# Convolution and pooling mixer of a two-block transformer kernel: taps accumulated in PSUM, three input groups on four banks, pooled channels first in the output product

## The reference

```python
def conv_pool_mixer(h, w_in, dw_w, dw_b, ln_g, ln_b, pool_w, pool_scale, w_out):
    z = h @ w_in                                   # 1024 -> 3 x 512
    a_val, a_gate, u = z[..., :512], z[..., 512:1024], z[..., 1024:]
    a = a_val * jax.nn.sigmoid(a_gate)
    a = causal_depthwise_conv(a, dw_w, 31 taps) + dw_b
    a = jax.nn.silu(layernorm(a, ln_g, ln_b))
    # u in 4 groups of 128 channels, windows 2, 4, 8, 16
    pooled = windowed_mean(u)                      # sum of the window / count
    p = einsum('btgc,gcd->btgd', pooled - u, pool_w) * pool_scale
    return jnp.concatenate([a, p], axis=-1) @ w_out   # 1024 -> 1024
```

## Time and profile before

| | us |
|---|---|
| median of 3 runs | 1901.66 |
| lowest and highest | 1900.48, 1903.46 |
| profiled execution, its own time | 1900.42 |
| its span in the trace | 1898.6 |
| PE busy | 1816.5 (96%) |
| DVE busy | 868.1 (46%) |
| ACT busy | 616.8 (32%) |
| POOL busy | 728.3 (38%) |

### The profile page before, as it was taken

The page is one execution under the profiler, slowest core; times in us unless marked ns, Lnnn a source line. Parts: engine busy times, 40 slices in busy tenths (PEclk is TensorE's granted clock), DMA queues, the critical chain, the costliest instruction groups (busy, mean ns, idle before and its releaser), DMA issues.

```text
span 1898.6 us, 24087 instructions
## 1 busy us (share of the span) xinstructions
PE 1816.5 (96%) x8442; PEld 1476.1 (78%) x8442; DVE 868.1 (46%) x1392; ACT 616.8 (32%) x814; POOL 728.3 (38%) x315
## 2 busy tenths in 40 slices
PE   8899989999999885999999999999999999999998
PEld 6788777888888773588888888888888788888886
DVE  2544446333333689642323324656657333242325
ACT  5444434222222430443222223434243342222223
POOL 3122224444444447245343544323233245444341
PEclk9899999999999997999999999999999999999999
DMA  9711112233232121033232323212122133323231
GB/s 199 121 56 56 56 56 89 89 99 102 97 99 93 61 74 56 20 103 100 78 110 88 106 93 93 84 46 77 55 66 66 45 111 100 99 88 99 79 109 45
DMA packets 149494, 159.78 MB, mean 84 GB/s; under 512 B 9892, under 2 KB 110872, under 8 KB 149440
## 3 DMA queue, kind: packets, MB, share of 16 engines
q1 hardware_dynamic: 148911, 158.79, 28.1%
q10 hardware_dynamic: 528, 0.26, 0.0%
HBM read 156.40 MB, written 2.62 MB: 84 GB/s over the span
## 4 chain that ended last, share of the span: by engine, by line
PE 49%; issue 29%; POOL 10%; DVE 7%; ACT 3%; DMA 1%; SPq 1%; POOLq 0%; DVEq 0%; ACTq 0%
PE ps L1017 43%; POOL wlo L562 10%; DVE conv L1822 3%; PE ps L1299 2%; PE ps L1166 1%; PE ps L1155 1%; DMA bias_rows<-relrow 1%; DVE ss L1498 1%; DVE acc L1519 0%; PE ps L1130 0%; PE ps L1131 0%; DVE h_lo L1486 0%; POOL wlo L573 0%; DMA raw<-in_w_in 0%; ACT whi L631 0%
## 5 line engine op out<-in xcount | busy, mean ns | idle before, releaser
L562 POOL TENSOR_TENSOR wlo<-raw,whi 128x1024 fp32r<-128x1024 f32 x272 | 657.6, 2431 | 1076.7 <-ACT whi L631 1062.8
L1017 PE MATMUL ps<-h_hi,wlo 128*128 128x512 f32 x1472 | 590.6, 401 | 15.8 <-POOL wlo L573 7.4
L1017 PE MATMUL ps<-h_hi,whi 128*128 128x512 f32 x1472 | 576.8, 392 | 0.0
L1017 PE MATMUL ps<-h_lo,whi 128*128 128x512 f32 x1472 | 575.7, 391 | 0.0
L631 ACT ACTIVATE whi<-raw 128x1024 fp32r<-128x1024 f32 x282 | 292.2, 1054 | 523.3 <-PE ps L1017 504.1
L1017 PEld LDWEIGHTS ps<-h_hi,wlo 128*128 128x128 f32 x1472 | 278.0, 189 | 79.1 <-POOL wlo L573 8.3
L1017 PE MATMUL ps<-m_hi,wlo 128*128 128x512 f32 x800 | 319.9, 400 | 4.2 <-DVE m_lo L1649 1.6
L1017 PEld LDWEIGHTS ps<-h_hi,whi 128*128 128x128 f32 x1472 | 277.3, 188 | 59.5
L1017 PEld LDWEIGHTS ps<-h_lo,whi 128*128 128x128 f32 x1472 | 278.1, 189 | 57.8 <-issue 2.9
L1017 PE MATMUL ps<-m_lo,whi 128*128 128x512 f32 x800 | 317.1, 396 | 0.0
L1017 PE MATMUL ps<-m_hi,whi 128*128 128x512 f32 x800 | 317.0, 396 | 0.0
(11 more groups left out here) (238 smaller groups left out, 1401.0 us busy)
## 6 DMA issues: line engine op xcount, KB each, us to landing
raw<-in_ffn_w SPq DMA_DIRECT2D x264, 256.0 KB, 2.9
raw<-in_w_ff SPq DMA_DIRECT2D x128, 256.0 KB, 2.9
raw<-in_hg_w_in SPq DMA_DIRECT2D x64, 256.0 KB, 3.3
raw<-in_w_in SPq DMA_DIRECT2D x40, 256.0 KB, 5.5
raw<-in_cp_w_in SPq DMA_DIRECT2D x24, 256.0 KB, 3.0
raw<-in_w_out SPq DMA_DIRECT2D x16, 256.0 KB, 2.9
raw<-in_cp_w_out SPq DMA_DIRECT2D x16, 256.0 KB, 2.9
raw<-in_hg_w_out SPq DMA_DIRECT2D x16, 256.0 KB, 2.8
```

The source lines that it names most:

```text
L562: pool.tensor_tensor(wlo[:, u % RING, :, :], raw[:, u % RING, :, :], whi[:, u % RING, :, :].bitcast(F32), ALU.subtract).then_inc(unit_lo, 1)
L1017: mm = pe.matmul(ps[:, b, :], wt[:, s, a, m * P:(m + 1) * P], xt[:, kts[a], :], start=starts and a == 0 and i == 0, stop=last)
```

## The change

In the mixer alone:

1. The taps of tiles 0, 1 and 2 accumulate in PSUM (banks 4, 5 and 6, the odd half sum of tile 2 in bank 4 once tile 0 is done): each step reads `apad` from SBUF and the running sum from PSUM, and writes to PSUM; the last step writes to `conv` in SBUF. As no PE or ACT instruction uses these banks meanwhile, DVE counts them up itself (`release`).
2. For that, the three input groups all use banks 0 to 3, in the order g = 0, 2, 1, and the tap matmuls and the variance use bank 7.
3. DVE takes the pooled input out one bank at a time ahead of steps 10 to 13, and the gates and values of group 1 tile by tile ahead of steps 24 to 29, tile 3 first; PE computes group 1 in the order 3, 1, 2, 0.
4. PE starts the taps of tile 3 when tile 3 alone is gated, does 16 taps, all four pool products, and the other 15; then output unit 0, the mean, output unit 1, the variance, and output units 2 to 7. `CPOUT_ORDER` puts all four units of pooled channels first, for both halves of the outputs, and SP loads in that order.
5. POOL does the low parts of units 8 to 11 before the windows, and of output units 0 to 2 after them. ACT splits one more unit before the first sigmoids, and scales the pool products before the bias of tile 3. The pool products are scaled into `pdiff` in place of the half of `late`, which still holds the tap matrices.

```diff
+CPOUT_ORDER = ((0, 4), (0, 6), (1, 4), (1, 6), (0, 0), (0, 2), (1, 0), (1, 2))
...
-    b.stage("cpin", [(("g", 0, m), m) for m in range(4)] + [(("g", 2, m), 4 + m) for m in range(4)]
-            + [(("g", 1, m), m) for m in range(4)] + [("conv", 4), ("mean", 5)]
-            + [(("pool", j), 6 + j % 2) for j in range(4)] + [("var", 4)])
+    b.stage("cpin", [(("g", g, m), m) for g in (0, 2, 1) for m in range(4)] + [(("pool", j), j) for j in range(4)]
+            + [(("taps", j), 4 + j) for j in range(3)] + [("odd", 4), ("mean", 5), ("conv", 7), ("var", 7)])
...
-            odd = sb("odd", [P, SEQ], scope=s)
...
-        csq, pout = late[:, 0:4, :], late[:, 4:8, :]
+        csq, pout = late[:, 0:4, :], pdiff
...
-            for h in range(2):
-                for j, kts in enumerate(order):
-                    load(U_CPOUT, 4 * h + j, pieces("cp_w_out_2", kts, h * COLS))
+            for j, (h, kt) in enumerate(CPOUT_ORDER):
+                load(U_CPOUT, j, pieces("cp_w_out_2", (kt, kt + 1), h * COLS))
...
-            lo_part(U_CPIN + 8)
-            lo_part(U_CPIN + 9)
+            for j in range(8, 12):
+                lo_part(U_CPIN + j)
...
-                if j < 3:
-                    lo_part(U_CPIN + 10 + j)
-            for j in range(1, 3):
+            for j in range(3):
                 lo_part(U_CPOUT + j)
...
             inv_rms(4)
-            for g in range(2):
-                if g:
-                    for j in range(4, 12):
-                        split(U_CPIN, j)
...
+            split(U_CPIN, 4)
+
+            def sigmoid_of(g, i):
+                b = banks.bank("cpin", ("g", g, 2 + i))
+                act.wait_ge(drained[b], nth("cpin", ("g", g, 2 + i)))
+                act.activation(csig[:, i, :], csig[:, i, :], ACT.Sigmoid).then_inc(csig_ready, 1)
+
+            sigmoid_of(0, 0)
+            sigmoid_of(0, 1)
+            for j in range(5, 12):
+                split(U_CPIN, j)
+            split(U_CPOUT, 0)
+            sigmoid_of(1, 1)
+            sigmoid_of(1, 0)
...
-            act.wait_ge(filled[4], nth("cpin", "conv"))
...
             for j in range(4):
                 pool_out(j)
             act.preload_act_table_set(LOG_TABLES)
+            act.wait_ge(filled[7], nth("cpin", "conv"))
+            c = COL["cp_dw_b_2"] + 3
+            act.activation(conv[:, 3, :], bank("cpin", "conv"), ACT.Identity, bias=vecs[:, c:c + 1])\
+                .then_inc(drained[7], 1)
+            split(U_CPOUT, 1)
...
-            split(U_CPOUT, 1)
-            act.wait_ge(filled[4], nth("cpin", "var"))
+            split(U_CPOUT, 2)
...
-                .then_inc(drained[4], 1)
-            act.wait_ge(drained[4], nth("cpin", "var"))
+                .then_inc(drained[7], 1)
+            act.wait_ge(drained[7], nth("cpin", "var"))
...
-            for j in range(2, 6):
+            for j in range(3, 6):
                 split(U_CPOUT, j)
...
-            gates_first = (2, 3, 0, 1)
-            group(U_CPIN, 0, "cpin", [("g", 0, m) for m in range(4)], order=gates_first, n=2, between=norm_after(4, 3))
+            group(U_CPIN, 0, "cpin", [("g", 0, m) for m in range(4)], order=(2, 3, 0, 1), n=2, between=norm_after(4, 3))
             group(U_CPIN, 4, "cpin", [("g", 2, m) for m in range(4)])
-            group(U_CPIN, 8, "cpin", [("g", 1, m) for m in range(4)], order=gates_first)
+            group(U_CPIN, 8, "cpin", [("g", 1, m) for m in range(4)], order=(3, 1, 2, 0))
...
+            def conv_taps(lo, hi):
+                for i in range(lo, hi):
+                    mm = pe.matmul(bank("cpin", "conv"), tapdiag[:, i, :], apad[:, 3, i:i + SEQ],
+                                   start=i == 0, stop=i == TAPS - 1)
+                    if i == TAPS - 1:
+                        mm.then_inc(filled[7], 1)
+
+            def cpout(j):
+                h, kt = CPOUT_ORDER[j]
...
+                unit(U_CPOUT, j, m_hi, m_lo, (kt, kt + 1), "cpout", [("h", h, m) for m in range(4)], kt == 4, kt == 2,
+                     wait_tile=tile if j in (4, 5) else None, by_tile=kt == 2)
+
+            pe.wait_ge(drained[7], before("cpin", "conv"))
+            pe.wait_ge(tapdiag_ready, 1)
+            pe.wait_ge(apad_ready, 3)
+            conv_taps(0, 16)
             pe.wait_ge(poolw_in, 16)
-            pool_product(0)
-            pool_product(1)
-
-            pe.wait_ge(drained[4], before("cpin", "conv"))
-            pe.wait_ge(tapdiag_ready, 1)
-            pe.wait_ge(apad_ready, 4)
-            for i in range(TAPS):
-                mm = pe.matmul(bank("cpin", "conv"), tapdiag[:, i, :], apad[:, 3, i:i + SEQ],
-                               start=i == 0, stop=i == TAPS - 1)
-            mm.then_inc(filled[4], 1)
+            for j in range(4):
+                pool_product(j)
+            conv_taps(16, TAPS)
+            pe.wait_ge(pout_lo, 2)
+            cpout(0)
             pe.wait_ge(drained[5], before("cpin", "mean"))
             pe.wait_ge(csum_step, 3)
             pe.matmul(bank("cpin", "mean"), ones[:, :], csum[:, :], start=True, stop=True).then_inc(filled[5], 1)
-            pool_product(2)
-            pool_product(3)
-            pe.wait_ge(pout_lo, 2)
-            out_unit(U_CPOUT, "cpout", 0)
-            pe.wait_ge(drained[4], before("cpin", "var"))
+            pe.wait_ge(pout_lo, 4)
+            cpout(1)
+            pe.wait_ge(drained[7], before("cpin", "var"))
             pe.wait_ge(csum_step, 6)
-            pe.matmul(bank("cpin", "var"), ones[:, :], csum[:, :], start=True, stop=True).then_inc(filled[4], 1)
-            pe.wait_ge(pout_lo, 4)
-            out_unit(U_CPOUT, "cpout", 1)
+            pe.matmul(bank("cpin", "var"), ones[:, :], csum[:, :], start=True, stop=True).then_inc(filled[7], 1)
             for j in range(2, 8):
-                if j < 4:
-                    pe.wait_ge(cs_lo, 2 * j - 2)
-                out_unit(U_CPOUT, "cpout", j)
+                cpout(j)
...
-            def gates(g):
...
-            def gated(g):
...
+            def gate_in(g, i):
+
+                b = banks.bank("cpin", ("g", g, 2 + i))
+                dve.wait_ge(filled[b], nth("cpin", ("g", g, 2 + i)))
+                dve.tensor_tensor(csig[:, i, :], ps[:, b, :], rs[:, :], ALU.mult).then_inc(drained[b], 1)
...
+            def value_in(g, i):
+
+                b = banks.bank("cpin", ("g", g, i))
+                dve.wait_ge(filled[b], nth("cpin", ("g", g, i)))
+                dve.tensor_tensor(apad[:, 2 * g + i, PAD:], ps[:, b, :], rs[:, :], ALU.mult).then_inc(drained[b], 1)
...
+            def gated(g, i, count):
+
+                b = banks.bank("cpin", ("g", g, i))
+                dve.wait_ge(drained[b], nth("cpin", ("g", g, i)))
+                dve.wait_ge(csig_ready, count)
+                dve.tensor_tensor(apad[:, 2 * g + i, PAD:], apad[:, 2 * g + i, PAD:], csig[:, i, :], ALU.mult)\
+                    .then_inc(apad_ready, 1)
...
+            def pool_in(m):
+                b = banks.bank("cpin", ("g", 2, m))
+                dve.wait_ge(filled[b], nth("cpin", ("g", 2, m)))
+                dve.tensor_tensor(upad[:, m, POOL_PAD:], ps[:, b, :], rs[:, :], ALU.mult).then_inc(drained[b], 1)
...
+            def release(b):
+
+                dve.sem_inc(filled[b], 1)
+                dve.sem_inc(drained[b], 1)
...
-                a, w_i = apad[:, j, i:i + SEQ], taps[:, i, j:j + 1]
+                a, w_i, b = apad[:, j, i:i + SEQ], taps[:, i, j:j + 1], banks.bank("cpin", ("taps", j))
                 if i == 0:
-                    dve.tensor_scalar(conv[:, j, :], a, w_i, col("cp_dw_b_2", j), ALU.mult, ALU.add)\
+                    dve.wait_ge(drained[b], before("cpin", ("taps", j)))
...
                     dve.wait_ge(tap_done[j], i)
-                    dve.scalar_tensor_tensor(out=conv[:, j, :], in0=a, scalar=w_i, in1=conv[:, j, :], op0=ALU.mult,
-                                             op1=ALU.add).then_inc(tap_done[j], 1)
-
...
+            gate_in(0, 0)
+            gate_in(0, 1)
+            value_in(0, 0)
+            value_in(0, 1)
+            gated(0, 0, 1)
+            gated(0, 1, 2)
...
             for i in range(TAPS):
-                if i == 13:
-
-                    for m in range(4):
-                        b = banks.bank("cpin", ("g", 2, m))
-                        dve.wait_ge(filled[b], nth("cpin", ("g", 2, m)))
-                        dve.tensor_tensor(upad[:, m, POOL_PAD:], ps[:, b, :], rs[:, :], ALU.mult).then_inc(drained[b], 1)
+                if 10 <= i < 14:
+                    pool_in(i - 10)
+                if i == 24:
+                    gate_in(1, 1)
+                if i == 25:
+                    value_in(1, 1)
                 if i == 26:
-                    gates(1)
+                    gate_in(1, 0)
                 if i == 27:
-                    gated(1)
+                    gated(1, 1, 3)
+                    value_in(1, 0)
+                if i == 29:
+                    gated(1, 0, 4)
                 tap(0, i)
```

(74 more changed lines are left out.)

14 lines of the change are left out of this document (5 added, 9 removed).

## The result

| us | before | after |
|---|---|---|
| median of 4 runs | 1902.23 (1900.48 to 1903.46) | **1879.78** (1878.69 to 1880.58) |
| profiled execution, its own time | 1900.42 | 1879.24 |
| its span | 1898.6 | 1877.5 |
| PE busy | 1816.5 | 1815.7 |
| DVE busy | 868.1 | 840.3 |

After takes 0.9882 of the time of before, 95% interval 0.9865 to 0.9899. The forecast was 1878, range 1872 to 1889. PE does the same work as before; it merely stands idle less.

A forecast was written before the change was run, and what follows sets the result against it. PE, busy 96%, was taken to bound the kernel, idling while DVE's taps took turns with POOL. GLU start moves from 831.30 to 807.5, gaining 23.8: 1900.4 becomes 1876.6, plus 1.2 for the median, forecast 1878 us, range 1872 to 1882.

The forecast's parts named there:

- (g): PE's clock falling after two new waits of 2.6 and 3.4 us: charged 1.6 and 1.8 us, end 807.5.
- p: Time between starts of two DVE tap steps in PSUM: taken as 0.66 us, bounds 0.60 and 1.35.
- Rival B: DVE steps slower, as reading and writing one bank might not stream together: p = 1.18, 1911 us; chance 0.06.
- C: DVE steps in between, p of 0.85 to 1.0: 1878 to 1892 us before any clock loss; chance 0.06.
- (a): Four banks for three groups: PE's pooled input waits for bank 0 until 677.3, ends at 699.2, 2.6 us later.
- (b): Pooled input taken out bank by bank: bank 3 free at 701.8, PE idles 2.6 us before group 1.
- (c): Gating tile 3, with 0.8 us for POOL: PE begins its taps at 727.0 instead of 750.35, idle 3.4 us.
- (d): PE's taps and products of tile 3: together 30.1 us, end 757.1; the output unit after them ends at 762.7.
- (e): DVE's work meanwhile: the mean could start at 758.7, before PE is ready; covered up to p = 0.79.
- (f): Mean to GLU: 41.4 us, the norm hidden by two pooled-channel units, without which PE would wait 10; end 804.1.
- Rival A: DVE's turns with POOL stay: mean near 780, gain 9 us less clock, 1893 us; chance 0.08.

The follow-up runs named there:

- after_again: The changed kernel as it is, run once more for comparison: 1879.83 us, ratio 0.988 to before.
- Kernel c: The changed kernel with ACT's split of output unit 4 put behind the inverse root: 1876.73 us, ratio 0.9861 to before.
- a: The changed kernel, taking the pooled input out ahead of and between the taps of two steps instead of four: 1879.09 us, ratio 0.987 to before.

## Why the prediction was right, and where its parts were not

All times from DVE's first take of a gate, as forecast (less 675.42) and as the trace of after has them:

| event | forecast | measured |
|---|---|---|
| first unit of the pooled input | 2.0 | 2.0 |
| group 1 starts | 26.4 | 26.6 |
| PE's taps of tile 3 start (clock charge of g in it) | 53.2 | 52.8 |
| mean | 90.7 | 88.7 |
| GLU starts | 132.1 | 131.5 |

**p, the step in PSUM.** I took 0.66 between 0.60 and 1.35. It is 0.66, and the bounds have their reasons now: 18 steps took 11.94 us in PSUM and 12.0 in SBUF (the first burst of the kernel with sums in SBUF, in which DVE was not held up). The clash was the second read, as the rows of line 1836 had suggested. Rival B (p over 1.08) and C (0.85 to 1.0) fell with this number. So did the estimate from the Trainium skill, Perfetto Trace Analysis, Optimizing Scalar/DVE Operations: its overhead for PSUM gives 0.73 to 0.79, the trace 0.66.

**(a) and (b)** hold to 0.2 us: first start, wait of 2.6 forecast and 2.54 measured, no low part late.

**(c)** I charged the gating of tile 3 with 0.8 for a clash with POOL. It took 0.68 us (729.03), because it began just ahead of POOL's mean, and POOL was held up:

```profile
729.11 1.95 POOL L594 TENSOR_SCALAR pmean<-wsum 128x512 f32<-128x512 f32 x1
```

The other three means took 1.49 us. In after_again the gating took 0.83 us. The wait was 2.5 for 3.4 (2.7 in after_again).

**(d) and (e)** hold: from the first tap to the end of output unit 0 35.9 us for 35.7, POOL's windows in 25 us (forecast: at most 30), PE didn't wait at the mean.

**(f) is the step that was short.** I let the norm from the mean to the GLU cost PE nothing but its own work, 41.4 us; it took 42.8. For the low parts of weights I had asked if they are in time, and not what they stand against: the one at 770.84 reads SBUF while DVE's last sum for the variance reads it twice, and two sums took 3.60 us. That made the 1.7 us of wait. Kernel c removed the wait and 1.7 us of stage. The other half of (f), that two more units of pooled channels hide the norm, held in kind. In size, I had said that PE would wait 10 us without them; with the old order it waited 5.1, as that 10.1 runs to the last low part of the norm and the unit needs its first tile first (in after the first low part ended 6.0 us after the variance began, the last 10.1).

**(g)** I charged 3.4 us for two falls of the clock. There was one, behind the second wait, about 1.6. The fall that is the most frequent I had not listed at all: it stands behind the first wait, 3.5 us for bank 0, which follows from (a) (0.87 of before and 2.6), and came in 10 of the 12 profiled executions with that wait, though not in this one. Up to the mean my sum was 2.0 too dear, from there on 1.4 too cheap; that the GLU came out only 0.6 early is owed to errors of opposite sign.

**Rival A was mis-sized.** I priced it at 1893, on the ground that the new order saves 9 us in what follows the mean. With the sums in SBUF the kernel took 1902.7: the turns of the earlier trace rows were not the law but one case of it. Where a low part came alone it was starved, the windows were pushed 18 us back, counted from the first gate, and they and the low parts behind them then stood against DVE's steps until 774 us; what the order saved went there. Had the PSUM operand not helped, the change would have made no difference, and my chance for that would have stood in the wrong place.

**Small slips in the sums.** By the rule that gave 1878 (1900.4 less the gain, plus 1.2) rival C comes to 1880 to 1894, not 1878 to 1892, and the low end to 1873, not 1872. Nothing hangs on it.

**Open:** what decides whether a POOL instruction that meets a burst is served at once or at its end. In before, one of line 573 at 687.40 us, inside a burst of DVE, took 2.51 us; in three kernels here one took 14.7. It is not how long POOL had been idle: in the kernel with the sums in SBUF one was starved after 4.11 us of idleness (690.65 above) and one served at once after 4.08, in the midst of tile 2's steps, one of which took 2.90 us:

```profile
777.51 2.71 POOL L572 TENSOR_TENSOR wlo<-raw,whi 128x1024 fp32r<-128x1024 f32 x1 [4.08 <-ACT whi L628]
```

I made no kernel that tells these apart. Nor is it shown why the clock falls behind a wait in one execution and not in the next.

## What to carry to other kernels

Where DVE and POOL work side by side for long, look at the operands: a DVE instruction that reads two tensors from SBUF stands against POOL, and moving one of them (a running sum lends itself) to a PSUM bank freed both here, at no cost to DVE (0.66 us a step for 0.67). Don't price such a clash with the mean rate of one stretch; it depends on how the two engines' instructions meet. And when a big wait has gone, read the waits of PE again: four of 1.7 to 3.5 us were left here, a few moved lines took three of them down or away, and small matmuls in the last kept the clock, for another 10 us in all.

## What the runs showed of the hardware that was not expected

- A POOL instruction of 2.4 us that met a burst of DVE steps with two SBUF reads took 14.7 us in three kernels, until some 2 us after the burst; an earlier one, in the burst of 18 steps, took 10 to 11 us in the same three.
- DVE can accumulate in place in a PSUM bank, reading and writing it in one instruction, at the pace of SBUF: 0.66 us for 512 columns of float32. The forecast took this value, but no row of before showed a write to PSUM.
- After a PE wait of 2.5 to 3.5 us the granted clock fell in some executions and not in others of the same kernel. The first wait was 3.5 us long in 12 profiled executions and the clock fell behind it in 10 (not in after and a). Behind the second and third wait, where they were 2.5 to 2.7 us, it fell once each (in after; in the kernel that writes to SBUF). Behind these waits and that of 5.1 us a fall cost 1.6 to 2.7 us: 8 to 14 matmuls that start 0.43 us apart, at the lower of the clock's two levels (1.2 GHz), instead of 0.23.
